# Up product of a decoder trunk: the sums of weights and rows move from GpSimd to VectorE

## The reference, cut to what matters

```python
x = x + jnp.einsum('nlc,cd->nld', mix, w['w_out'])
u = jnp.einsum('nld,df->nlf', rmsnorm(x, w['norm2_g']), w['mlp_up'])
x = x + jnp.einsum('nlf,fd->nld', jnp.square(jax.nn.relu(u)), w['mlp_down'])
```

## Time and profile before

| | |
|---|---|
| profiled execution | 3189.1 us |
| its span | 3187.0 us |
| median of three runs | 3192.96 us |
| DVE busy | 1868.6 us (59%) |
| ACT busy | 830.2 us (26%) |
| POOL busy | 712.6 us (22%) |

### The profile page before, as it was taken

The page is one execution under the profiler, slowest core; times in us unless marked ns, Lnnn a source line. Parts: engine busy times, 40 slices in busy tenths (PEclk is TensorE's granted clock), DMA queues, the critical chain, the costliest instruction groups (busy, mean ns, idle before and its releaser), DMA issues. The chain is left out here.

```text
span 3187.0 us, 64433 instructions
## 1 busy us (share of the span) xinstructions
PE 2972.6 (93%) x27272; PEld 2585.3 (81%) x27272; DVE 1868.6 (59%) x3164; ACT 830.2 (26%) x1315; POOL 712.6 (22%) x689
## 2 busy tenths in 40 slices
PE   7999999799878888886899999998999999999998
PEld 7999998556567777785688898998999877777776
DVE  6211111477566666654345778878878666666667
ACT  5000000365423233323124333333332111110113
POOL 4000000364232233220001446446452000000000
PEclk9999999899989999996799999999999999999999
DMA  4121221442132221102266433433435212122212
GB/s 156 69 74 65 74 72 60 117 131 72 55 128 77 95 80 65 40 8 79 93 192 183 161 134 124 146 130 116 146 133 211 108 67 81 55 79 67 81 54 107
DMA packets 164715, 317.69 MB, mean 100 GB/s; under 512 B 26016, under 2 KB 105376, under 8 KB 157792
## 3 DMA queue, kind: packets, MB, share of 16 engines
q1 hardware_dynamic: 164448, 313.84, 29.1%
HBM read 219.20 MB, written 94.60 MB: 98 GB/s over the span
## 5 line engine op out<-in xcount | busy, mean ns | idle before, releaser
L2674 PE MATMUL m_bank<-m_hh,m_wuh 128*128 128x348 f32 (+1 forms) x1344 | 436.8, 325 | 34.6 <-DVE m_hl L2875 20.5
L2675 PE MATMUL m_bank<-m_hl,m_wuh 128*128 128x348 f32 (+1 forms) x1344 | 436.3, 325 | 0.0
L189 PE MATMUL p_bank<-p_xh,p_wh 128*128 128x416 f32 x800 | 286.5, 358 | 11.5 <-DVE p_wl L310 11.5
L2674 PEld LDWEIGHTS m_bank<-m_hh,m_wuh 128*128 128x128 f32 x1344 | 256.3, 191 | 37.2 <-issue 29.6
L190 PE MATMUL p_bank<-p_xl,p_wh 128*128 128x416 f32 x800 | 283.8, 355 | 0.0
L191 PE MATMUL p_bank<-p_xh,p_wl 128*128 128x416 f32 x800 | 282.8, 353 | 0.0
L2941 DVE TENSOR_TENSOR m_y_low<-m_y_low,m_bank 128x512 f32<-128x512 f32 x288 | 194.8, 686 | 140.3 <-PE m_bank L2676 136.5
L2675 PEld LDWEIGHTS m_bank<-m_hl,m_wuh 128*128 128x128 f32 x1344 | 256.6, 191 | 0.0
L2676 PE MATMUL m_bank<-m_hh,m_wsl 128*128 128x348 f32 (+1 forms) x768 | 249.2, 325 | 0.0
L2941 DVE TENSOR_TENSOR m_mix<-m_mix,m_bank 128x512 f32<-128x512 f32 x224 | 152.1, 686 | 117.6 <-PE m_bank L2676 116.4
L2676 PE MATMUL m_bank<-m_wuh,m_wul 128*128 128x512 f32 x512 | 200.9, 392 | 0.0
(11 more groups left out here) (439 smaller groups left out, 6967.1 us busy)
## 6 DMA issues: line engine op xcount, KB each, us to landing
m_wur<-w_up SPq DMA_DIRECT2D x48, 1024.0 KB, 4.9
m_wur<-uT SPq DMA_DIRECT2D x24, 1024.0 KB, 5.2
p_ring<-units SPq DMA_DIRECT2D x30, 768.0 KB, 6.1
uT<-m_u SPq DMA_DIRECT2D x32, 696.0 KB, 3.2
out_projT<-p_ob SPq DMA_DIRECT2D x100, 208.0 KB, 1.9
cp_z<-out_projT SPq DMA_DIRECT2D x8, 1408.0 KB, 7.6
uT<-m_u SPq DMA_DIRECT2D x16, 688.0 KB, 3.2
p_wr<-w_fm SPq DMA_DIRECT2D x20, 512.0 KB, 3.7
```

Of the source, the lines that this page charges most:

```text
L189: pe.matmul(out, wh_, mh, start=(k == 0), stop=False)
L2674: pe.matmul(out, wh_, mh, start=first, stop=False)
L2675: pe.matmul(out, wh_, ml, start=False, stop=False)
```

## The change

1. The four sums of weights of a unit (`sums`), the four sums of rows of a chunk (`mix`) and of the first chunk (`first_mix`) run on DVE. POOL has no instruction left in the output projection and in the MLP.
2. The row sums get places of their own: T1 in the place of the rows B12, T2 and T3 in a new tile `more`, T4 in `more` and one block of `rows`. They no longer wait for products, and are computed one at a time in units 5 to 8 of the chunk before (`MIX_AT`). T4 lies in two pieces, so its sum and its split are two instructions.
3. The sums of unit 0 are computed in the output projection (`first_sums`), into the staging tile. At the start of the MLP the split is done in three parts (`first_high`, `first_low`): block A11, then the four sums, then A12 and A22. These stand ahead of `add` on DVE and ahead of `norm` on ACT, and PE waits for each part separately.
4. ACT no longer copies P5. DVE adds it to both sums straight from its bank (`join_5`).
5. DVE's order within a unit changes: the last join and squaring of unit q-1 (`join_3`) stand at the head of unit q, then `sums(q+1)`, `low_a(q+1)`, a row sum where there is one, `join_6_7`, `low_s(q+1)`, `join_2`, `join_5`, `join_4`. At an edge the splits of rows stand between them.

```diff
@@ first chunk and first unit, inside out_project @@
-    def first_mix(self, pool, k):
+    def first_mix(self, dve, k):
...
+    def first_sums(self, dve):
+        a21, a11, a12, a22 = (self.wa0[0][:, i * KH * P:(i + 1) * KH * P] for i in range(4))
+        s1, s2, s3, s4 = (self.s0[:, i * KH * P:(i + 1) * KH * P] for i in range(4))
+        dve.wait_ge(self.h_low, 3 * KH)
+        dve.wait_ge(self.wu_in[0], 16)
...
                 if 0 <= t - FIRST_AT < KH:
+                    hand.first_mix(dve, t - FIRST_AT)
                     hand.first_low(dve, t - FIRST_AT)
+                if t == FIRST_AT + KH:
+                    hand.first_sums(dve)
@@ places of the row sums @@
+            return {B11: [of[:, 0:KH, 0:n]], T1: [of[:, 0:KH, n:2 * n]],
+                    B21: [of[:, KH:KC, 0:n]], B22: [of[:, KH:KC, n:2 * n]],
+                    T2: [spare(more, 0, n, KH)], T3: [spare(more, PART, n, KH)],
+                    T4: [spare(more, 2 * PART, n, KH - 1), spare(rows, 2 * KC * NC, n, 1)]}
+        MIX_AT = 5
@@ tensor: waits of a product @@
+                if q == 0:
+                    if p == 0:
+                        pe.wait_ge(a11_low, 1)
                         pe.wait_ge(hand.h_low, fresh_done(1))
+                    if p == 1:
+                        pe.wait_ge(w_low, 1)
+                    if p == 3:
+                        pe.wait_ge(w_low, 2)
@@ scalar @@
+            def first_high():
+                act.activation(wslot(wh[0], A11), wslot(wa[0][0], 1), ACT.Copy).then_inc(a11_high, 1)
+                act.activation(wslot(wh[0], S1, 4), hand.s0, ACT.Copy).then_inc(w_high, 1)
+                act.activation(wslot(wh[0], A12, 2), wslot(wa[0][0], 2, 2), ACT.Copy).then_inc(w_high, 1)
...
-                snap(q, P1)
                 if begun:
                     high_h(begun, 5)
+                snap(q)
...
-                snap(q, P5)
@@ vector: new joins of the bank of P5 @@
+            def join_5(q):
+                dve.wait_ge(p_done, NPR * q + P5 + 1)
+                dve.wait_ge(joined, NJ * q + 2)
+                join(q, 1, 1, P5)
+                join(q, 3, 2, P5)
@@ vector: the loop over q @@
+                if begun:
+                    join_4(q - 1)
+                    join_3(q - 1)
+                    low_h(begun, 5)
+                    low_h(begun, 6)
+                elif q:
+                    join_3(q - 1)
                 if q + 1 < NUP:
-                    low_a(q + 1)
+                    sums(q + 1)
...
+                if begun:
+                    join_6_7(q)
+                if q + 1 < NUP:
+                    low_a(q + 1)
+                c, i = divmod(q, FP)
+                if c + 1 < len(CHUNKS) and 0 <= i - MIX_AT < 4:
+                    mix(c + 1, i - MIX_AT)
                 if edge:
                     low_h(edge, 0)
-                join_first(q)
+                if not begun:
+                    join_6_7(q)
...
@@ gpsimd: the whole block of mlp goes @@
-            sums(0)
-            for q in range(NUP):
-                if q + 1 < NUP:
-                    sums(q + 1)
-                if (q + 1) % FP == 0 and q + 1 < NUP:
-                    mix((q + 1) // FP)
```

More of the change, by code:

```diff
@@ L2857, in _, with first_low, sums, mix @@
         def _(dve):
+            def first_low():
+                raw, low = wa[0]
+                high = lambda i, m: wslot(wh[0], i, m).bitcast(F32)
+                dve.wait_ge(a11_high, 1)
+                dve.tensor_tensor(wslot(low, 1), wslot(raw, 1), high(A11, 1), ALU.subtract).then_inc(a11_low, 1)
+                dve.wait_ge(w_high, 1)
+                dve.tensor_tensor(ws[0][1][:, :], hand.s0, high(S1, 4), ALU.subtract).then_inc(w_low, 1)
+                dve.wait_ge(w_high, 2)
+                dve.tensor_tensor(wslot(low, 2, 2), wslot(raw, 2, 2), high(A12, 2), ALU.subtract).then_inc(w_low, 1)
+            def sums(q):
+                a21, a11, a12, a22 = (wslot(wa[q % 3][0], i) for i in range(4))
+                s1, s2, s3, s4 = (wslot(ws[q % 2][0], i) for i in range(4))
+                dve.wait_ge(wu_in[q % 3], 16 * (q // 3 + 1))
+                if q >= 2:
+                    dve.wait_ge(p_done, NPR * (q - 1))
+                dve.tensor_tensor(s1, a21, a22, ALU.add).then_inc(summed, 1)
+                dve.tensor_tensor(s3, a11, a21, ALU.subtract).then_inc(summed, 1)
+                dve.wait_ge(summed, 4 * q + 1)
+                dve.tensor_tensor(s2, s1, a11, ALU.subtract).then_inc(summed, 1)
+                dve.wait_ge(summed, 4 * q + 3)
+                dve.tensor_tensor(s4, a12, s2, ALU.subtract).then_inc(summed, 1)
+            def mix(c, i):
+                f = fresh(c)
+                at = 4 * (KH + c - 1)
+                if i == 0:
+                    dve.wait_ge(h_in, 32 * c)
+                else:
+                    dve.wait_ge(hand.mixed, at + i)
+                to, left, right, op = [(T3, B22, T1, ALU.subtract), (T1, T1, B11, ALU.subtract),
+                                       (T2, T3, B11, ALU.add), (T4, B21, T2, ALU.subtract)][i]
+                parts = f[to]
+                for out, x, z in zip(parts, split(f[left][0], parts), split(f[right][0], parts)):
+                    m = dve.tensor_tensor(out, x, z, op)
+                m.then_inc(hand.mixed, 1)
             def low_a(q):
@@ L2957, in normalise @@
                                          op0=ALU.mult, op1=ALU.mult).then_inc(normed, 1)
+            first_low()
             hand.add(dve, hand.NT - 1)
             hand.invert(dve, hand.NT - 1)
-            low_a(0)
-            low_s(0)
             hand.copy_out(dve, hand.NT - 2)
```

178 lines of the change are left out of this document (77 added, 101 removed).

## The result

The changed kernel takes 3153.14 us (median of four runs, 3147.85 to 3161.07) against 3189.15 us (median of four runs of the kernel before): 36.0 us less, ratio 0.9889 with a 95% interval of 0.9859 to 0.9919. Run once more beside the later experiments (e11) its ratio was 0.9875, 0.9849 to 0.9901. The profiled execution took 3150.39 us with a span of 3148.6 us, 38.4 us under the span before.

What follows compares the result with a forecast made beforehand. PE bounds the kernel mid-chunk, losing time at edges and start. Gains of 28.2 (edges) and 5.2 us (start) sum to 33.4, giving 3155.7 from the profiled run or 3159.6 from the median; forecast 3158 us, range 3147 to 3174.

Steps and rivals of the forecast that it cites:

- What bounds: Up product: PE is full mid-chunk; it loses 37.4 us at the two chunk edges and 8.5 us at the start.
- The unit on DVE: Mid-chunk unit: DVE needs 12.0 us of 13.39, 90%, so PE stays the bound; bounds 11.4 to 14.4 us.
- The edge: Chunk edges: walking DVE's queue leaves PE waiting 3.0 us at unit 17; gain 28.2 us over two edges, bounds 13 to 33.
- the clock: Half-clock matmuls after PE waits: 1.6 us charged at each edge, and 0.8 us at the start.
- The start: Behind the barrier: first product 6.6 us earlier, second waits 1.5, last tile's transposes 0.5; gain 5.2 us, bounds 3 to 6.6.
- Row sums mid-chunk: Units 5 to 8 of two chunks: DVE falls back 0.8 us, hidden, cost nothing; without cover 6.4 us a chunk.
- the output projection: Four tiles with `first_mix`: 2.0 us more on DVE, margin 1.4 us, cost nothing; `first_sums` likewise.
- P5: Up product units: adding P5 straight from its bank, without ACT's copy, changes nothing.
- SP: Order unchanged; at an edge the store of unit 15 waits until 21.0 instead of about 15 us, costing nothing.
- the down product: Its start waits for the last join as before, so it costs nothing.
- The explanation of the edges: Chunk edges: POOL does the row sums late, after products free their places, and slows DVE's splits, 4.54 against 1.59 us.
- The rule that spoke against the change: Trainium skill: with DVE saturated, move work off it; applies only if the unit exceeded 13.39 us.

Runs made afterwards that it cites:

- e11: The changed kernel run again, unedited, on the same chip as e10; ratio 0.9875 to the kernel before, from transposes to first down product 651.6 us.
- e5: Changed kernel plus four unread 128x256 DVE additions in each of units 2 to 39; from transposes to first down product 679.9 us against 651.6.
- e4: Changed kernel plus two unread 128x256 DVE additions in each of units 2 to 39; from transposes to first down product 653.6 us against 651.6.
- e10: Changed kernel with edge squarings behind low_s and join_5, and unit 0's split in five parts; median 3141.56 us, ratio 0.9852 to the kernel before.
- e9: Changed kernel with ACT copying P5 out of its bank again; from transposes to first down product 651.9 us against 651.6.
- e8: Changed kernel with weight sums and mid-chunk row sums on POOL, first sums still on DVE; from transposes to first down product 658.6 us against 651.6.
- e3: Changed kernel with all four row sums on DVE in units 15 and 31; from transposes to first down product 668.7 us against 651.6.
- e6: Changed kernel with unit 0's sums on DVE behind the barrier, ahead of A11's split; from transposes to first down product 655.3 us against 651.6.
- e7: Changed kernel with the squarings of units 15 and 31 behind low_a of units 17 and 33; transposes to first down product 649.9 us against 651.6.
- e2: Changed kernel with the row sums on POOL, still mid-chunk in units 5 to 8; from transposes to first down product 651.6 us against 651.6.
- e1: Changed kernel with the weight sums of units 1 to 47 back on POOL; from transposes to first down product 657.1 us against 651.6.

## Why the prediction was right, step by step

The forecast of 3158 us lies 5 us above the measured 3153.14. That is nearer than the whole times can be trusted, since the four runs lie 13 us apart; the fairer test is the gain, put at 33.4 us and 37.6 in the stretch.

*What bounds.* Right: PE mid-chunk, DVE's queue at the edges and at the start.

*The unit on DVE.* 12.0 us forecast, 11.7 by e5 and 11.9 by the two waits. A sum 0.67 forecast, 0.68 measured; a squaring 0.95 with its wait, 0.88 and 0.03. The prediction reads "1.80 us and more" for the squarings of before; of the two in its unit one took 1.80 us and the other 1.44. The interpolation between subtractions of other lengths held, and the limit too: e4 stays below it, e5 crosses it.

*The edge.* The walk through the queue can be laid beside the trace, counted from the start of unit 15 at 1960.89:

```profile
1965.17 1.76 DVE L2929 TENSOR_TENSOR m_wul<-m_wur,m_wuh 128x1536 fp32r<-128x1536 f32 x1
...
1970.86 2.28 DVE L2934 TENSOR_TENSOR m_wsl<-m_wsr,m_wuh 128x2048 fp32r<-128x2048 f32 x1
...
1980.78 0.88 DVE L2987 SCALAR_TENSOR_TENSOR m_u<-m_stage 128x696 f32<-128x696 f32 x1
1981.58 1.24 DVE L2942 TENSOR_TENSOR m_hl<-m_more,m_hh 128x1044 fp32r<-128x1044 f32 x1
...
1988.20 1.75 DVE L2929 TENSOR_TENSOR m_wul<-m_wur,m_wuh 128x1536 fp32r<-128x1536 f32 x1
```

low_a ends at 6.0 (forecast 5.9), low_s at 12.3 (12.2), the last squaring at 20.8 (21.0), low_a of unit 17 at 29.1 (29.6). PE waits for it 2.19 us (2.7), which is named where the walk put it:

```profile
1990.01 0.43 PE L2693 MATMUL m_bank<-m_hh,m_wuh 128*128 128x348 f32 x1 [2.19 <-DVE m_wul L2929]
```

*The mis-sized term: the clock.* I had charged 1.6 us of half clock at each edge and 0.8 at the start, 4.0 in all. Of the three places only the second edge had one: unit 33 took 14.86 us there and 13.64 at full clock (e10), 1.2 us. That is 2.8 of the 4.2 us by which the gain was too small in my sum. The rest is spread: without the clock both edges came to 5.5 us instead of 6.0, the start gave 0.3 us more, the kernel before had lost 37.8 us at its edges and not 37.4, and unit 45 gave 0.3.

*The start.* First product 1.5 us behind the barrier forecast; it comes 1.24 us after the transposes begin, as these rows show, and the second waits 1.23 us (1.5). The wait for the last tile's `copy_out` is 0.19 us (0.5).

```profile
1755.92 1.06 PE L2320 MATMUL m_bank<-p_ident,m_rows 128*128 128x128 f32 x8 [0.47 <-PEq L2411]
1757.16 0.42 PE L2693 MATMUL m_bank<-m_hh,m_wuh 128*128 128x348 f32 x1 [0.18 <-DVE m_wul L2892]
1760.57 0.43 PE L2693 MATMUL m_bank<-m_hh,m_wuh 128*128 128x348 f32 x1 [1.23 <-DVE m_wsl L2894]
```

*Row sums mid-chunk, the output projection, P5, SP, the down product.* Each was put at nothing. Units 6 to 10 take 13.38 to 13.39 us, e9 gives 0.3 us for P5, and the part behind the first down product is 741.0 and 741.1 us. In the output projection the transposes of one tile follow those of the tile before by 11.77 to 11.81 us in both kernels, the four tiles with `first_mix` and the one with `first_sums` included, and from 1560 us to the barrier the profile lists no wait of PE in either.

*The explanation of the edges* was too simple in one point. I named POOL's slowing of DVE and the late row sums together. e8 and e3 part them: with the sums of units and chunks on POOL, but the row sums early, 25.8 of the 31.1 us at the edges are won; with POOL empty, but the row sums at the edge, 17.1 are lost again. The moment of the row sums is the larger cause, and the places of their own allow it. The parts are not independent, so they don't add up to the whole. Two things are not parted by any run. The new order of DVE (and of ACT) at the edges is in e3 and in e8 alike, so some of the 25.8 us may be its own. Of the 6.3 us at the start e6 gives 3.7 to the first sums ahead of the barrier; the rest, the split in three parts and its place ahead of `add`, was not tried alone.

*The rule that spoke against the change* did not come to bear: DVE rose from 77% to 86% in plain units and 94% in a window with row sums. The 0.9 us more of e4 did not saturate it, the 1.7 us more of e5 did.

## What to carry to other kernels

Before work is moved to another engine, write down that engine's queue between two places where the matmul engine must be fed, with durations from rows at which no neighbour interferes, and check each due time behind the moved item, not only the first one (e7). Work that needs only early inputs belongs in the units with slack, and a buffer of its own is what buys this. For the row sums the moment was worth 17.1 us here (e3), and the engine, once they stood mid-chunk, nothing (e2). A change of 0.2% can be judged by a stretch between two fixed events of the trace where total times can't, if the stretch repeats, as it did here to 0.04 us.

## What the runs showed of the hardware

- A DVE instruction with two operands in SBUF stands still while POOL executes one: 3.85 us instead of 0.88 beside an instruction of 3.19 us (e2). The Trainium skill says the same (SBUF — State Buffer, "SBUF: two separate sides"): the shared pair of ports is an exclusive lock, and whichever starts first has it for the whole instruction. The trace agrees: POOL starts 0.08 us earlier, and the squaring ends 0.74 us after POOL. Additions with one operand in PSUM were not slowed (0.50 and 0.51 us in e1).
- Whether a wait of PE brings half clock isn't told by its length alone: the waits of 2.19 and 2.21 us of the changed kernel had none and one; e4's 2.56 and 0.81 us close together had none at either edge; e6's 2.13 and 0.99 us had 6.8 us of it. It is not chance alone either: in all five profiles with these edges (the changed kernel's two, e2, e6, e9) the first edge has no half clock and the second has 3.4 us. What tells the two edges apart stays open.
- Equal code ahead of the barrier took up to 17.7 us longer in one execution than in another (1750.62 and 1768.33), while the stretch behind it was the same to 0.04 us in the changed kernel's two profiles. The granted clock goes with it: ahead of the transposes its records have 164 us at half clock in e3 and 205 in e2, and over the thirteen profiles the two go together (160 to 205 us at half clock, correlation 0.96). Why the clock differs there was not tried.
